# Writing the gated one-hot rows of a dense mixture gate on GpSimd alone, per token

## The reference

```python
sv, si = lax.top_k(scores, PEER_TOPK)
cand = sv[..., 0, :, None] + sv[..., 1, None, :]
cv, ci = lax.top_k(cand.reshape(t, PEER_HEADS, PEER_TOPK * PEER_TOPK), PEER_TOPK)
i1 = jnp.take_along_axis(si[..., 0, :], ci // PEER_TOPK, axis=-1)
i2 = jnp.take_along_axis(si[..., 1, :], ci % PEER_TOPK, axis=-1)
gates = jax.nn.softmax(cv, axis=-1)
act = jax.nn.gelu(jnp.einsum('tkd,td->tk', expert_u[eb], xb))
out = jnp.einsum('tk,tkd->td', act * gb, expert_v[eb])
```

## Time and profile before

| | |
|---|---|
| median of 3 runs | 5057.75 us (5054.53 to 5059.38) |
| the profiled execution | 5062.22 us |
| its span in the profile | 5060.4 us |
| PE busy over the span | 4256.8 us (84%) |
| DVE busy | 2735.3 us (54%) |
| POOL busy | 593.9 us (12%) |
| granted TensorE clock, mean | 0.909 |

### The profile page before, as it was taken

One profiled execution on the slowest core, in us unless ns is written; L12 is line 12 of the kernel. 1 busy time (PEld: TensorE's weight loads), 2 busy tenths in 40 slices (PEclk: granted clock), 3 DMA queues, 4 the chain that ended last, 5 costly groups with the idle time before them and its releaser, 6 DMA issues. The chain is left out here.

```text
span 5060.4 us, 52602 instructions
## 1 busy us (share of the span) xinstructions
PE 4256.8 (84%) x20559; PEld 3569.1 (71%) x20559; DVE 2735.3 (54%) x4312; ACT 1446.5 (29%) x2204; POOL 593.9 (12%) x393
## 2 busy tenths in 40 slices
PE   7995794579889899999879878598998977767998
PEld 5883693468888799999758635377877854446886
DVE  3223674549998876777632256644333225665343
ACT  2221222323233333333222115233222211613322
POOL 0000001000555563333100000000000000000000
PEclk8997896789899999999989978799999987878999
DMA  3442004333678689999634310132323421022232
GB/s 109 143 141 84 1 1 129 109 108 119 206 249 309 233 277 324 335 347 349 224 100 143 103 59 1 36 133 75 100 91 110 141 80 59 1 71 98 92 99 77
DMA packets 333850, 691.47 MB, mean 137 GB/s; under 512 B 24067, under 2 KB 89091, under 8 KB 332332
## 3 DMA queue, kind: packets, MB, share of 16 engines
q1 hardware_dynamic: 256380, 466.98, 28.4%
q0 software_dynamic: 36864, 134.23, 7.7%
q10 hardware_dynamic: 40368, 87.04, 4.5%
HBM read 583.04 MB, written 105.14 MB: 136 GB/s over the span
## 5 line engine op out<-in xcount | busy, mean ns | idle before, releaser
L310 DVE TENSOR_TENSOR in_w_low<-in_w,in_w_high 128x512 fp32r<-128x512 f32 x344 | 214.5, 686 | 650.8 <-ACT in_w_high L304 650.8
L354 PE MATMUL ps<-xn_high,in_w_high 128*128 128x512 f32 x1056 | 414.7, 393 | 51.0 <-DVE in_w_low L310 51.0
L1699 PE MATMUL ps<-xn_p_high,pe_w_high 128*128 128x384 f32 (+1 forms) x1152 | 411.4, 357 | 46.2 <-DVE pe_w_low L1872 46.2
L354 PE MATMUL ps<-xn_high,in_w_low 128*128 128x512 f32 x1056 | 414.1, 392 | 0.0
L354 PE MATMUL ps<-xn_low,in_w_high 128*128 128x512 f32 x1056 | 413.6, 392 | 0.0
L1699 PE MATMUL ps<-xn_p_high,pe_w_low 128*128 128x384 f32 (+1 forms) x1152 | 401.0, 348 | 0.0
L1699 PE MATMUL ps<-xn_p_low,pe_w_high 128*128 128x384 f32 (+1 forms) x1152 | 400.2, 347 | 0.0
L1872 DVE TENSOR_TENSOR pe_w_low<-pe_w_raw,pe_w_high 128x2048 fp32r<-128x2048 f32 x136 | 329.9, 2427 | 106.1 <-ACT pe_w_high L1806 105.7
L1806 ACT CAST pe_w_high<-pe_w_raw 128x2048 fp32r<-128x2048 f32 x136 | 259.4, 1909 | 419.0 <-DMA pe_w_raw<-in_peer_v 223.7
L310 DVE TENSOR_TENSOR mlp_w_low<-mlp_w,mlp_w_high 128x512 fp32r<-128x512 f32 x256 | 159.7, 686 | 369.1 <-ACT mlp_w_high L304 369.1
L1729 PE MATMUL ps<-pe_far_hidden_high,pe_w_high 128*128 128x384 f32 x1024 | 346.0, 338 | 14.1 <-DVE pe_near_hl L1999 13.9
(11 more groups left out here) (533 smaller groups left out, 9282.0 us busy)
## 6 DMA issues: line engine op xcount, KB each, us to landing
in_w<-in_w_in SPq DMA_DIRECT2D x86, 1024.0 KB, 6.1
pe_w_raw<-in_peer_uT SPq DMA_DIRECT2D x64, 1024.0 KB
pe_w_raw<-in_peer_v SPq DMA_DIRECT2D x64, 1024.0 KB
dram_pf<-in_out ACTq DMA_DIRECT2D x33, 1024.0 KB, 8.3
mlp_w<-in_w_up SPq DMA_DIRECT2D x32, 1024.0 KB, 5.3
mlp_w<-in_w_down SPq DMA_DIRECT2D x32, 1024.0 KB, 5.0
dram_peer_hidden<-pe_rings_r ACTq DMA_DIRECT2D x64, 384.0 KB
dram_peer_gates<-pe_near_gate_out SPq DMA_DIRECT2D x6, 4096.0 KB, 17.9
```

What stands on the lines that cost most here:

```text
L310: dve.tensor_tensor(lo[:, s, c, :], raw[:, s, c, :], hi[:, s, c, :].bitcast(F32), ALU.subtract).then_inc(lo_done, 1)
L354: last = pe.matmul(k.ps[:, 4 * parity + q, :], a, b, start=(i == 0 and c == 0 and p == 0), stop=(i == upg - 1 and c == UC - 1 and p == 2))
L1699: last = pe.matmul(ps[:, q, 0:n], w[:, s, at], xp[:, 4 * i + c, 0:n], start=(i == 0 and c == 0 and p == 0), stop=(i == 1 and c == 3 and p ...
```

## The change

DVE no longer writes I. POOL writes it from `iota`, the first key and the gate, one instruction for each token: compare with the key, multiply by the gate, both taken as scalars of a partition. That makes eight POOL instructions of 128x128 in an iteration instead of two of 128x512. The semaphore `one_i` goes; POOL waits itself for the turned keys (`kept_T`) and for the ring (`gate_made`). The due time of POOL's halves goes from GATE + 2 and + 4 to GATE + 1 and + 3, and that of J from GATE + 2 to GATE.

```diff
--- before.py
+++ after.py
@@ -1582,7 +1582,7 @@
     pick, c_val_a, c_cut, c_val_b, c_top = (sem(n) for n in ("pick", "c_val_a", "c_cut", "c_val_b", "c_top"))
     shifted, raised, hot, picked, ready, turned, kept_T = (sem(n) for n in ("shifted", "raised", "hot", "picked", "ready",
                                                                            "turned", "kept_T"))
-    one_i, one_j, gated, gate_made, gate_kept, gate_stored = (sem(n) for n in ("one_i", "one_j", "gated", "gate_made",
+    one_j, gated, gate_made, gate_kept, gate_stored = (sem(n) for n in ("one_j", "gated", "gate_made",
                                                                                "gate_kept", "gate_stored"))
     h_in, g_in = [sem(f"h_in{s}") for s in range(3)], [sem(f"g_in{s}") for s in range(3)]
     h_scaled, h_hi, h_lo, summed = (sem(n) for n in ("h_scaled", "h_hi", "h_lo", "summed"))
@@ -1978,12 +1978,9 @@
                         if it >= RING:
 
                             dve.wait_ge(gate_made, 2 * (it - RING + 1))
-                        for c, to, done in ((0, I_[s], one_i), (1, J[s], one_j)):
-                            if c == 1:
-                                yield GATE(it) + 2.0
-                            keys = keyT[:, c, it * UNIT:(it + 1) * UNIT]
-                            dve.tensor_tensor(to, iota[:, :].unsqueeze(1).to_broadcast(full), keys.unsqueeze(2).to_broadcast(full),
-                                              ALU.is_equal).then_inc(done, 1)
+                        keys = keyT[:, 1, it * UNIT:(it + 1) * UNIT]
+                        dve.tensor_tensor(J[s], iota[:, :].unsqueeze(1).to_broadcast(full), keys.unsqueeze(2).to_broadcast(full),
+                                          ALU.is_equal).then_inc(one_j, 1)
 
                 def hidden_split():
                     for e in range(N_DOWN + 1):
@@ -2051,13 +2048,16 @@
                 def gates():
                     for it in range(n_gates):
                         for o in range(2):
-                            yield GATE(it) + 2.0 + 2.0 * o
+                            yield GATE(it) + 1.0 + 2.0 * o
                             if o == 0:
-                                pool.wait_ge(one_i, it + 1)
-                            n = 2 * it + o
-                            to = I_[it % RING][:, 4 * o:4 * o + 4, :]
-                            pool.tensor_tensor(to, to, gateT[:, 4 * n:4 * n + 4].unsqueeze(2).to_broadcast([P, 4, P]),
-                                               ALU.mult).then_inc(gated, 1)
+                                pool.wait_ge(kept_T, 2 * (TURNED.index(it // 16) + 1))
+                                if it >= RING:
+                                    pool.wait_ge(gate_made, 2 * (it - RING + 1))
+                            for j in range(4 * o, 4 * o + 4):
+                                t = it * UNIT + j
+                                last = pool.tensor_scalar(I_[it % RING][:, j, :], iota[:, :], keyT[:, 0, t:t + 1], gateT[:, t:t + 1],
+                                                          ALU.is_equal, ALU.mult)
+                            last.then_inc(gated, 1)
 
                 def gathers():
                     for n in range(2 * PASSES):
```

## The result

The change is slower: a median of 5228.66 us (5224.68 to 5235.42, four runs) against 5058.57 us of the kernel before, ratio 1.0335 with a 95% interval of 1.0317 to 1.0353. The profiled execution took 5227.22 us with a span of 5225.4 us, 165 us more than before. I had predicted 5043 us, in a range up to 5110.

What follows compares the result with a forecast made beforehand. PE's 61 us of waits before its gate products, with DVE the bound in the second and fourth group, was the most to win; 13.7 us of new waits less 29 gained gave -15, so 5043 us, range 4998 to 5110.

Steps and rivals of the forecast that it cites:

- The bound and the floor: Gate-matrix stage: PE idles 60.8 us before its gate products (L1792), the most to win; its dense products are the floor.
- x: Time of one POOL compare-and-multiply of 128x128 with two scalars per partition: taken as 0.43 us, 0.23 and 1.04 kept.
- rival C: Gating before L1792: POOL becomes the bound from about 0.49 us an instruction, slower, 5105 us at 0.65; chance 0.33.
- The pace of POOL: POOL's iteration in the stage: 9.04 us against PE's 8.47, giving 13.7 us of new waits before the gate products.
- 8x + 5.6: POOL's iteration in us: eight instructions, 2.2 for two gathers, 3.4 of waits; counted in four groups DVE does not bound.
- The gain: Stage: 29 us, 10 each in the second and fourth group from DVE's relief, 9 in fifth and sixth from earlier J.
- The moved gather: POOL's order: the first half of I ahead of a gather delays it by 4x plus waits; costed at nothing, three rows spare.
- The Trainium skill's price for a scalar: POOL's instruction: about 102 cycles a small read, two scalars 0.17 us, instruction about 0.50 us, sum at no change.
- My price of DVE's disturbance: POOL holding up DVE in an iteration: 3.8 x 0.43 = 1.6 us after against two blockings of 0.84 us before, equal.

Runs made afterwards that it cites:

- order_only: Kernel before the change, with J right behind I and POOL's halves due one us earlier: 5045.29 us, ratio 0.997 to the kernel before.
- one_wide: The changed kernel, each half of I made by one POOL compare-and-multiply of 128x512 with constants instead of four of 128x128: 5045.42 us, ratio 0.997.
- dve_tokens: The changed kernel, with the compare-and-multiply for each token on DVE instead of POOL: 5041.21 us, ratio 0.9957 to the kernel before.
- act_gate: Kernel before in the change's order, DVE making I wide and ACT instead of POOL multiplying by the gates token by token: 5023.52 us, ratio 0.992.
- due_back: The changed kernel with the due times of before (POOL at 2 and 4, J at 2): 5239.96 us, ratio 1.0359 to the kernel before.

## Why the prediction was wrong

**The bound and the floor** held: the loss is in the stage and in front of L1792, and PE's pace where nothing holds it is 8.44 us an iteration in order_only, one_wide, dve_tokens and act_gate alike (8.47 in the earlier trace rows). What I called the floor is one only at a given clock.

**The step that failed is the size of x.** I took 0.43 us, by a copy's and a multiply's rate and 98 ns for two scalars, and kept 0.23 to 1.04. It is 0.78. The row to which I scaled is of another form, a multiply of two tensors, and that form takes 453 ns at 128x128; the form with scalars takes 605 ns even with one operation and one scalar. The start with its scalars is 0.39 us instead of my 0.20, and the 128 elements are 0.40 us (788 ns less the start) instead of 0.23. The range was then cut at x = 0.65, though the bounds that I had from the rows reached to 1.04: with an unmeasured instruction that runs 384 times, that was too sure. My rival C named the place and the sign, with a chance of 0.33.

**The pace of POOL** has x as its largest term: 8x was 3.4 us at my x and is 6.2 us at 0.78. With x = 0.78 the formula 8x + 5.6 gives 11.8 us; measured were 12.68 in the change and 12.33 in due_back. That it fell short by under one us is in the waits: 1222 - 780 = 442 ns an instruction, 3.5 us an iteration, as much as I had put down for all of POOL's waits, gathers included. The formula would have given 24 x 3.4 = 80 us of new waits in the four groups and none in the second and fourth. The rows show 102 us of idle time over all six.

**What the formula had no term for** is the clock. 58 of the 160 us are PE being busy longer, at a granted clock of 0.88 instead of 0.94: more of the stretch, behind the short stops, at the lower of its two levels (1.2 instead of 2.4 GHz). I had counted only how long PE stands, never how it runs afterwards. In act_gate, where PE waits 25 us in front of L1792, the clock is 0.96.

**The gain.** I counted 10 us for each DVE-bound group and 9 for J ahead of late weights. The second was right in kind, by order_only: it gains 0.3% and takes the waits at L1792 from 60.8 to 35.2 us. DVE's relief alone gave nothing that could be told from it (one_wide).

**The moved gather** I had cost at nothing. In order it is harmless (order_only), but with a full POOL its cover is gone: DVE waited for rows 25 times. The move is not the cause either: in due_back, where it is taken back, DVE still waits for rows 20 times, 85 us instead of 103, and the time is no lower.

**The Trainium skill's price for a scalar** in GPSIMD Engine Reference, section Performance pitfalls for Q7 kernels, about 102 cycles for a read command, was nearer than mine: two scalars cost 147 ns, where I had worked out 0.17 us from it and put down 0.10 by my rows. The Trainium skill's other rule, in section Engine selection of the same page, that one-input work runs at about line rate there, does not hold for this instruction: 3.3 ns an element against 0.83 of the copy.

**My price of DVE's disturbance** (two multiplies' turns before, 3.8 x after) was wrong in DVE's favour: DVE hardly loses anything to the three-read form; it is POOL that waits.

## What to carry to other kernels

Measure a POOL instruction that a change issues hundreds of times, in its exact form, before believing a sum: at the same 128x128 the forms took from 0.29 to 0.79 us, and the one that was needed was nearly twice as dear as the rates of neighbours said. Where an in-order engine is fed by a second one, count the second one's whole iteration, waits included, against the pace of the first; once it is over, every iteration pays, and here the slower clock of PE added more than half as much again (58 us to 102). Work that waits on POOL beside DVE may be better off on an engine that has idle time and is not held up by DVE, here ACT, whose 384 multiplies all took 384 to 411 ns.

## What the runs showed of the hardware

- On POOL a compare-and-multiply costs 3.3 ns an element and about 0.39 us to start with two scalars; an addition in place of the comparison makes 128x128 0.34 us cheaper, yet a multiply alone with one scalar takes 608 ns and a compare alone 605 ns; the copy of 128x128 takes 289 ns.
- Taking turns between DVE and POOL is not symmetrical. A POOL multiply of 128x512 nearly doubles the time of a DVE subtraction beside it (25.44 us for twelve, against 13.7); a compare-and-multiply of 128x128 with two scalars takes 3.6 us beside them and costs DVE 2%. The Trainium skill, in SBUF — State Buffer, section Who interferes with whom, says of the ports that the two engines share that "it's an exclusive lock". That agrees with the multiply. A lock held by POOL for a whole instruction would not agree with the compare-and-multiply of 128x512: it takes 2.08 us undisturbed, and twelve DVE instructions beside it lost only 14.95 - 13.7 = 1.3 us together.
- On DVE the same compare-and-multiply of 128x128 takes 0.34 us in the median (dve_tokens), less than half of POOL's, and on ACT a multiply by one scalar takes 0.39 us (act_gate).
- TensorE fell to the lower level of its clock (granted 0.50) behind a stop of 3.86 us, and eight gate products took 2.05 us there instead of 1.05.
